# Scattering one more expert group before the last tile sums: one group instead of two added on chip

## What is computed

```
scores = sigmoid(t @ w_router)                     # 384 x 64
idx = top_k(scores + b_router, 8)
combine = one_hot(idx) * scores[idx] / sum * 2.5    # 384 x 64
act = silu(t @ w_gate_e) * (t @ w_up_e) * combine   # 64 experts of 1024 x 256
routed = sum over experts of act @ w_down_e         # 256 x 1024
x = x + g2 * (routed + shared expert);  y = rmsnorm(x) * final_norm_w
```

## Time and profile before

| | |
|---|---|
| median of 3 runs | 1029.17 us (1026.71 to 1030.17) |
| the profiled execution | 1028.87 us, span 1027.1 us |
| mean granted clock of the matrix engine | 0.974 of full speed |
| busy share of the span | PE 91%, PE weight loads 47%, DVE 29%, ACT 17%, POOL 10% |
| DMA | 324.26 MB, 316 GB/s mean |

### The profile page before, as it was taken

The page is one execution under the profiler, slowest core; times in us unless marked ns, Lnnn a source line. Parts: engine busy times, 40 slices in busy tenths (PEclk is TensorE's granted clock), DMA queues, the critical chain, the costliest instruction groups (busy, mean ns, idle before and its releaser), DMA issues.

```text
span 1027.1 us, 12887 instructions
## 1 busy us (share of the span) xinstructions
PE 934.2 (91%) x4925; PEld 480.9 (47%) x4925; DVE 300.2 (29%) x575; ACT 171.6 (17%) x281; POOL 106.2 (10%) x207
## 2 busy tenths in 40 slices
PE   4899899999999999999999999999898898979784
PEld 0455456677555568744444343434243343334332
DVE  2408713136300324441123221222112111212147
ACT  2131230112001002202111111111111111111111
POOL 2000000000000000020112121112121111112100
PEclk8899999999999999999999999999999899999998
DMA  9745466521364349799999999999999999999993
GB/s 375 261 164 205 159 235 219 160 87 54 114 225 144 121 161 421 313 390 364 367 365 419 420 420 420 420 420 420 419 421 420 421 421 421 420 421 420 422 419 164
DMA packets 82687, 324.26 MB, mean 316 GB/s; under 512 B 10650, under 2 KB 39494, under 8 KB 52672
## 3 DMA queue, kind: packets, MB, share of 16 engines
q1 hardware_dynamic: 66864, 289.43, 70.6%
q0 software_dynamic: 10368, 24.45, 6.1%
q10 hardware_dynamic: 5392, 9.52, 2.6%
HBM read 302.05 MB, written 34.64 MB: 328 GB/s over the span
## 4 chain that ended last, share of the span: by engine, by line
PE 77%; DVE 10%; DMA 5%; ACT 4%; issue 3%; SPq 0%; DVEq 0%; POOLq 0%; ACTq 0%
PE bank L514 25%; PE bank L1633 17%; PE bank L543 12%; PE bank L1785 4%; PE bank L1772 4%; PE bank L501 3%; DMA arena<-in_w_mod_dram 2%; ACT arena L525 2%; DMA arena<-expert_rows 2%; PE bank L1692 2%; DVE arena L528 2%; PE bank L1812 2%; PE bank L532 1%; PE bank L1618 1%; DVE arena L1078 1%
## 5 line engine op out<-in xcount | busy, mean ns | idle before, releaser
L514 PE MATMUL bank<-arena 128*32 128x512 f32 (+2 forms) x1536 | 269.7, 607 | 22.6 <-issue 21.5
L1633 PE MATMUL bank<-arena 128*128 128x384 f32 x640 | 211.2, 491 | 4.7 <-DVE arena L1023 4.7
L514 PEld LDWEIGHTS bank<-arena 128*32 128x32 f32 (+2 forms) x1536 | 92.0, 127 | 197.0 <-issue 197.0
L1633 PEld LDWEIGHTS bank<-arena 128*128 128x128 f32 x640 | 121.7, 192 | 96.5 <-issue 9.4
L543 PE MATMUL bank<-arena 128*32 128x512 f32 (+2 forms) x768 | 134.4, 596 | 0.6 <-issue 0.6
L543 PEld LDWEIGHTS bank<-arena 128*32 128x32 f32 (+2 forms) x768 | 41.3, 124 | 66.9 <-issue 66.9
L528 DVE TENSOR_TENSOR arena<-arena,bank 128x256 f32<-128x256 f32 x37 | 22.2, 600 | 170.1 <-ACT arena L525 170.1
L525 ACT ACTIVATE arena<-bank 128x256 f32<-128x256 f32 x37 | 22.8, 615 | 264.3 <-PE bank L514 264.3
L488 POOL DMA_INDIRECT arena<-h_rows,arena x37 | 39.0, 1055 | 248.7 <-issue 128.9
L548 DVE TENSOR_SCALAR arena<-bank,arena 128x512 f32<-128x512 f32 x37 | 27.8, 751 | 104.1 <-PE bank L543 104.1
L494 POOL DMA_INDIRECT expert_rows<-arena x35 | 35.9, 1025 | 163.0 <-DVE arena L548 163.0
(11 more groups left out here) (243 smaller groups left out, 671.7 us busy)
## 6 DMA issues: line engine op xcount, KB each, us to landing
arena<-in_w_gate_e_dram SPq DMA_DIRECT2D x64, 1024.0 KB, 24.4
arena<-in_w_up_e_dram SPq DMA_DIRECT2D x64, 1024.0 KB, 28.5
arena<-in_w_down_e_dram SPq DMA_DIRECT2D x64, 1024.0 KB, 28.4
arena<-in_w_mod_dram SPq DMA_DIRECT2D x24, 1024.0 KB, 8.2
arena<-in_w_in_dram SPq DMA_DIRECT2D x22, 1024.0 KB, 5.6
expert_rows<-arena SPq DMA_DIRECT2D x6, 2048.0 KB, 23.5
arena<-expert_rows SPq DMA_DIRECT2D x12, 1024.0 KB, 24.5
arena<-mod_rows_out ACTq DMA_DIRECT2D x4, 1024.0 KB, 8.8
```

What stands on the lines that cost most here:

```text
L514: ins = pe.matmul(bank[off:off + width, :], x_T[:, k, off:off + width], w[:, :, k, :], start=(k == 0), stop=(k == KT - 1))
L1633: ins = pe.matmul(ps[:, 0:TOK], w[:, k, P * (n % 2):P * (n % 2) + P], hT[:, k, :], start=(k == 0), stop=(k == KT - 1))
```

## The change

The last group alone is added on the chip (`ADDED` = 36); group 35 is scattered as the others are. So there is one 0/1 product to a tile half instead of two. For tile 2 the matrix engine adds three pieces (12 identity products) instead of two, and waits for the high pieces too before it begins them. POOL makes `token_no` before it waits for the scatters, not after. The vector engine loads the spill count in the last turn of its loop over groups and not where `spill` stands. The waits of SP are written by `NQ`, and ask for the same counts as before.

```diff
-ADDED = NQ - 2
-SUM_FROM = [0, 2, 2]
+ADDED = NQ - 1
+SUM_FROM = [0, 2, 3]
...
-        def spill(eng, body):
-
+        def most_left(eng):
             eng.wait_ge(S["tokens_ready"], 1)
-            most = eng.value_load(most_i[0:1, 0:1], min_val=0, max_val=TOK)
+            return eng.value_load(most_i[0:1, 0:1], min_val=0, max_val=TOK)
+
+        def spill(eng, body, most=None):
+            if most is None:
+                most = most_left(eng)
...
             scatter(ADDED - 1)
-            for b in range(2):
-                pool.wait_ge(x["scattered"][b], 16 * ((ADDED + 1 - b) // 2))
-            pool.sem_inc(S["moe_done"], 1)
             pool.wait_ge(x["xtr_done"], ADDED + 1)
             link(pool.iota(token_no.bitcast(I32), pattern=[[1, TOK]], base=0, channel_multiplier=0))
             link(pool.tensor_copy(token_no, token_no.bitcast(I32)))
             pool.sem_inc(S["token_no_ready"], 1)
+            for b in range(2):
+                pool.wait_ge(x["scattered"][b], 16 * ((ADDED + 1 - b) // 2))
+            pool.sem_inc(S["moe_done"], 1)
             spill(pool, pool_spill)
...
                 if i == NQ - 1:
+                    most = most_left(dve)
                     dve.wait_ge(S["token_no_ready"], 1)
-                    for n in range(2):
+                    for n in range(NQ - ADDED):
                         dve.tensor_scalar(places[n], token_no, token_of[:, n:n + 1], None, ALU.is_equal)\
                             .then_inc(S["places_ready"], 1)
...
-            sp.wait_ge(X[0]["y_done"], ADDED)
+            sp.wait_ge(X[0]["y_done"], NQ - 2)
             for n in range(4 * NT):
                 if n == 6:
-                    sp.wait_ge(X[0]["y_done"], ADDED + 1)
+                    sp.wait_ge(X[0]["y_done"], NQ - 1)
                 read_piece(sp, n)
...
             for t in range(NT):
-                for n in range(2):
+                for n in range(NQ - ADDED):
                     pe.wait_ge(S["places_ready"], n + 1)
...
                 if SUM_FROM[t]:
                     pe.wait_ge(low_rows_in[t], 32)
+                    if SUM_FROM[t] > 2:
+                        pe.wait_ge(high_rows_in[t], 32)
```

More of the change, by code:

```diff
@@ L795, in dve_loop @@
                     link(dve.tensor_tensor(x1[:, i - 4, :], x1[:, i - 4, :], y_shared[:, i - 4, :], ALU.add))
+            return most
         all_rows = rows_dram.rearrange("(t p k) d -> t p k d", p=P, k=TOPK)
@@ L1269, in vector_part_b @@
             dve.sem_inc(S["tokens_ready"], 1)
-            dve_loop(dve, X[0], link, one_hot, numbers, x_half)
+            most = dve_loop(dve, X[0], link, one_hot, numbers, x_half)
             dve.wait_ge(high_rows_in[0], 32)
@@ L1275, in vector_part_b @@
             dve.sem_inc(S["first_tile_summed"], 1)
-            spill(dve, dve_spill)
+            spill(dve, dve_spill, most)
             def joined(t):
@@ L1886, in _ @@
                                         y_e[(ADDED + n) % 2][:, 512 * i:512 * i + 512], start=(n == 0),
-                                        stop=(SUM_FROM[t] == 0 and n == 1))
+                                        stop=(SUM_FROM[t] == 0 and ADDED + n == NQ - 1))
                 if SUM_FROM[t]:
                     pe.wait_ge(low_rows_in[t], 32)
+                    if SUM_FROM[t] > 2:
+                        pe.wait_ge(high_rows_in[t], 32)
                     for i in range(2):
```

## The result

| | before | after |
|---|---|---|
| median | 1027.94 us (1026.59 to 1030.17, 4 runs) | 1038.26 us (1038.08 to 1039.09, 4 runs) |
| profiled execution | 1028.87, span 1027.1 | 1038.19, span 1036.5 |
| share of the chain | PE 77%, DVE 10%, DMA 5% | PE 79%, DVE 8%, DMA 6% |

The changed kernel takes 1.0093 times as long, 95% interval 1.0073 to 1.0113: some 9.6 us slower, against a forecast of 11.5 and a range of 1034.0 to 1044.7. Two far slower executions, one of e_sum2 (3832 us) and one of e_half_piece (1248 us), are left out of the ratios.

A forecast was written before the change was run, and what follows sets the result against it. The prediction took the tail as bound by a landing, then vector work. Late read 4.1, sums behind the last read 4.8 and clock 2.6 made it 11.5 us slower, 1040.7 us, range 1034.0 to 1044.7.

The forecast's parts named there:

- Group 35 scattered, and the reads held for it: Tail: scatter 35 takes 5.7 us, first read issued at 981.6, last read lands at 1015.2, 4.1 us later than before.
- The rule weighed against it: Scatter 35: the skill's fit, 2.0 us plus bytes over 436e3 per us, gives 3.2 us and a time of about 1038.2.
- Sums of tile 2 on the matrix engine: Tile 2's tail: 24 instructions, 10.7 us, all run behind the last read; 4.8 us of the loss.
- The granted clock: Tile 2's sums on the matrix engine: slowed by the lower clock after idling, 2.6 us added, bounds 0 and some 3.
- The vector engine: Last join: ready by 1018.9, then waits about 10 us; the wait hides a saving of up to 3.3 us.
- Token numbers, the add ahead of the weighting, SP's waits: POOL, vector engine and SP in the tail: token numbers have 5 us of slack, the later add and SP's waits cost nothing.
- The sum: Whole kernel: sums done at 1028.6 plus a 10.0 us tail, span 1038.6, time 1040.7 us, 11.5 slower.
- The scatter takes its usual time: Scatter 35: rival with the median 8.4 us, time 1043.4, or 1044.7 with 9.7 us; chance 0.18.
- The reads aren't late: Tail reads: rival in which the last lands near 1011.1 and only the sums cost, 1034.0 or 1036.6; chance 0.10.
- faster: Join of tile 2: rival in which the vector engine remains the bound, saving 3.3 us, 1025.9; chance 0.04.
- it does little: Tail: rival in which faster reads, overlapping sums and the gains eat most of the loss, within 0.3%; chance 0.04.
- the clock stays up: Tile 2's sums: rival without the clock's 2.6 us, or with a scatter faster than any seen, 1038.1; chance 0.14.

The follow-up runs named there:

- e_sum2: The changed kernel with tile 2's sums as before (matrix engine adds two pieces, vector engine the other two): 1.0037 of the kernel before, 3.8 us slower.
- e_half_piece: e_moves_only with half of piece 10 added by the matrix engine, the three other halves of pieces 10 and 11 by the vector engine: 0.9985 of the kernel before.
- e_warm: The changed kernel with four spare products ahead of the wait for tile 2's high pieces: one execution, 1036.77 us; block of 24 instructions 10.57 us.
- e_sum3_only: The kernel before, two groups still added on chip, with the matrix engine adding three pieces of tile 2 behind a wait for all four: 1.0051, 5.2 us slower.
- e_split: The changed kernel with the wait for tile 2's high pieces moved behind the eight products of the low ones: 1.0038 of the kernel before, 3.9 us slower.
- e_moves_only: The kernel before with only token numbers ahead of POOL's wait and the spill count loaded in the vector engine's last turn: 0.9984 of the kernel before.

## Why the prediction was right

*Group 35 scattered, and the reads held for it.* Right in kind, and a little small: 4.1 us forecast, 5.0 in the table. Counted from W = 952.1, the forecast had the weighting of group 35 done at 22.8, the scatter issued at 23.7 and landed at 29.4, 5.7 us later. In the changed kernel these are 970.8 - 950.1 = 20.7, then 21.5 and 29.0: the scatter took 7.43 us. Of the 2.1 us by which the weighting came sooner, 1.7 is one block of group 35's matmuls, which took 8.78 us in the execution read for the forecast, its granted clock at 0.50 from 960 to 963, and 7.09 in this one. So two errors of some 2 us cancelled, and the first read was forecast to half a us with luck. In the four kernels that scatter group 35 the first read goes out 29.0 or 29.1 us behind W, though the scatter is issued at 971.64 - 950.1 = 21.5 in three and at 975.28 - 953.0 = 22.3 in e_sum2. That fits a scatter that lands with the last of the weights (in the kernel before, the last load of weights landed 28.1 behind W), whenever it was issued; no run tests it by itself. From first issue to second landing the forecast had 7.6 us; the first add begins 986.91 - 979.13 = 7.8 behind it. The row for it was less idle than the forecast said, with 385 GB/s in the us ahead of the load at 375.1. From the second to the last landing it had 26.0; it was 27.2. That stretch is the mis-sized term, and why it is longer stays open.

*The rule weighed against it.* The Trainium skill's fit for a scatter of this size ("DMA: Bandwidth & Descriptors", the section on a DMA issued by GpSimd) gave an estimate of 3.2 us and a time of 1038.2, near what was measured. The time is no support for it: the scatters here took 6.6 to 7.5 us, issued while weights still flowed, and the nearness comes from other terms. No run shows a scatter on idle engines.

*Sums of tile 2 on the matrix engine.* Right in place and size. 10.7 us forecast at the upper clock, 10.57 in e_warm; e_sum3_only shows it with the reads early, e_split shows that the wait's place makes it cost.

*The granted clock.* The term was oversized: 2.6 us forecast from a block behind 4.29 us of idle time, 1.4 to 1.5 measured behind 4.43. The row chosen ran 5 us at the 1.2 GHz level; here the granted clock was 0.50 from 1014 and up again within the fourth us. The matrix engine had been idle for 4.43 us, where the sum had 6.0. The forecast also took tile 1's sums at the upper clock, 7.1 us; they took 8.83 behind 3.80 us of idle time. That cost nothing, since the last landing was still to come.

*The vector engine.* Right: ready at 1017.4, it waited 8.96 us (10 forecast), and the 3.3 us taken off its line did nothing. That they would be worth up to 3.3 us without the wait is too much: in e_moves_only the load's 1.0 us brings 0.3 behind the last landing (15.7 against 16.0).

*Token numbers, the add ahead of the weighting, SP's waits.* Right: the comparison was done at 974.2, 8.4 us before the product, and the matrix engine's 0/1 products, begun at 990.09, were over before the landing at 999.25.

*The sum*: 11.5 forecast, 11.4 in the table, 10.3 between the medians and 9.6 by the ratio. The landing was forecast 0.9 too small and what is behind it 1.0 too large (7.4 against 6.4), and the two cancel: that the total is right to 0.1 in the table is luck.

*The rivals.* "The scatter takes its usual time" was half right, 7.43 us, but its price didn't follow, since the scatter was also issued 2.2 us sooner, counted from W, than forecast. "The reads aren't late", "faster" and "it does little" fell: none of their conditions was met. For "the clock stays up" e_warm shows what it would have been.

What stays open: why the stream of weights runs up to 4.8 us earlier or later (W from 948.5 to 953.3 in the ten profiles, in no order that the edits explain).

## What to carry to other kernels

Here reads issued into a full queue had slack up to the moment at which the queue would have run empty: issuing them 6 us later moved the last landing by 0.1 us, and in the runs past that moment it came a fixed 35 us behind the first issue. So find that moment before moving the issue of a transfer. When work is moved from a busy engine to an idle one behind the last input, put each wait directly ahead of what needs it; a joint wait held 16 instructions back that needed none of what it waited for. And where the taking engine then finishes behind the giving one, as in e_split, the move has gained nothing.

## What the runs showed that was not expected

- A scatter issued while the weights' queue drains seems to land with the drain: four kernels, issue from 21.5 to 22.3 us behind W, first read always 29.0 to 29.1 behind W. The issues lie only 0.8 us apart, so this is a pattern and not a test.
- The last landing is the same to 0.1 us counted from the last issue of weights in the five kernels with early reads (59.0 to 59.1), whether the first read goes out 14.9 or 22.7 us behind it.
- The price of an idle stretch of the matrix engine isn't a function of its length alone. Against the same blocks at the upper clock: 2.13 us idle cost 8 instructions 1.8 us (5.36 against 3.60), 3.80 cost 16 of them 1.7 (8.83 against 7.13), 4.34 and 4.43 cost 24 of them 1.7 and 1.5 (12.23 and 12.11 against 10.57), and 4.29 cost 32 matmuls of a group 2.6.
